# Routing tiles 0 to 3 early, so that expert 0's first block runs in fp32 beside the rest of the routing

## The reference

```
hx = rmsnorm(x) * (1 + scale1) + shift1        # adaLN; the same for the context
x  = x + gate1 * (concat(pool_mixer, gated_linear_attention) @ w_out)
hx = rmsnorm(x) * (1 + scale2) + shift2
s  = sigmoid(hx @ w_router)                    # 16 experts in 4 groups of 4
# the group with the best pair sum of s + router_bias is chosen, and in it the best 2 experts
dest: the token-expert pairs sorted by expert, each expert padded to whole blocks of 128 rows
for each block b of expert e:
    yb = (silu(xb @ w1[e]) * (xb @ w3[e])) @ w2[e]     # w1, w3: 1024 x 512; w2: 512 x 1024
x  = x + gate2 * (sum of a token's two rows of yb, weighted by s of the chosen two)
out = rmsnorm(x) * norm_f
```

## Time and profile before

| | us |
|---|---|
| median of three runs | 888.96 |
| the profiled execution | 889.26 |
| its span, from first to last instruction | 887.50 |
| PE busy (share of span) | 858.4 (97%) |
| DVE busy | 636.0 (72%) |
| ACT busy | 414.9 (47%) |
| POOL busy | 192.3 (22%) |
| mean granted clock of PE | 0.986 |

### The profile page before, as it was taken

How to read it: one execution, slowest core, us unless ns; L and a number is a source line. 1 busy time by engine, 2 the same in 40 slices (tenths; PEclk the granted TensorE clock), 3 DMA queues, 4 the chain that set the end, 5 groups by cost and what they waited for, 6 DMA issues and landing times.

```text
span 887.5 us, 14102 instructions
## 1 busy us (share of the span) xinstructions
PE 858.4 (97%) x4980; PEld 706.4 (80%) x4981; DVE 636.0 (72%) x907; ACT 414.9 (47%) x597; POOL 192.3 (22%) x225
## 2 busy tenths in 40 slices
PE   8999999999999999999799999999999999999993
PEld 6789878888997567887688888888888888888872
DVE  1578755789777748556985669399936648599995
ACT  3585456201224442222343456378634525487772
POOL 4042001100000101011032324133413222234324
PEclk9999999999999999999979999999999999999997
DMA  9953566511035032322789859979997596599994
GB/s 342 347 180 111 172 196 203 163 41 54 11 143 191 1 143 78 113 73 95 259 304 375 277 171 368 285 269 378 378 346 265 176 299 220 175 348 379 370 333 175
DMA packets 82358, 195.29 MB, mean 220 GB/s; under 512 B 4919, under 2 KB 13324, under 8 KB 82314
## 3 DMA queue, kind: packets, MB, share of 16 engines
q1 hardware_dynamic: 71168, 158.87, 50.2%
q0 software_dynamic: 8272, 25.84, 11.2%
q10 hardware_dynamic: 2874, 10.01, 2.9%
HBM read 169.57 MB, written 25.71 MB: 220 GB/s over the span
## 4 chain that ended last, share of the span: by engine, by line
PE 78%; DVE 11%; DMA 4%; issue 2%; ACT 2%; POOL 1%; ACTq 0%; SPq 0%; DVEq 0%; POOLq 0%
PE ps L2455 17%; PE ps L2443 12%; PE ps L2108 9%; PE ps L2460 8%; PE ps L2111 7%; PE ps L2437 2%; PE ps L2308 2%; DMA raw<-in_w_dram 2%; PE ps L2299 1%; DMA raw<-x_rows 1%; DVE arena L1423 1%; PE ps L2301 1%; PE ps L2300 1%; PE ps L2250 1%; PE ps L2164 1%
## 5 line engine op out<-in xcount | busy, mean ns | idle before, releaser
L1145 ACT ACTIVATE wah<-raw 128x2048 fp32r (+1 forms) x32 | 61.4, 1919 | 63.7 <-PE ps L2460 42.4
L1856 DVE TENSOR_TENSOR wbl<-raw,wbh 128x2048 fp32r<-128x2048 f32 x32 | 73.1, 2288 | 5.3 <-ACT wbh L1145 4.9
L2443 PE MATMUL ps<-w2h,hTh 128*128 128x512 f32 x184 | 76.1, 414 | 0.0
L2455 PE MATMUL ps<-wbh,xTh 128*128 128x512 f32 x184 | 73.9, 402 | 0.0
L2455 PE MATMUL ps<-wah,xTh 128*128 128x512 f32 x184 | 72.6, 394 | 0.0
L2443 PE MATMUL ps<-w2h,hTl 128*128 128x512 f32 x184 | 72.2, 393 | 0.0
L2455 PE MATMUL ps<-wal,xTh 128*128 128x512 f32 x184 | 72.2, 392 | 0.0
L776 POOL DMA_INDIRECT x_rows<-late_rows,block_dst x21 | 49.9, 2375 | 102.7 <-DVE late_rows L1871 102.7
L2443 PE MATMUL ps<-w2l,hTh 128*128 128x512 f32 x184 | 72.1, 392 | 0.0
L1856 DVE TENSOR_TENSOR wal<-raw,wah 128x2048 fp32r<-128x2048 f32 x30 | 68.8, 2292 | 4.5 <-issue 3.2
L1856 DVE TENSOR_TENSOR w2l<-raw,w2h 128x2048 fp32r<-128x2048 f32 x32 | 71.8, 2283 | 0.0
(11 more groups left out here) (412 smaller groups left out, 2173.8 us busy)
## 6 DMA issues: line engine op xcount, KB each, us to landing
raw<-in_w_dram SPq DMA_DIRECT2D x64, 1024.0 KB
raw<-in_w_dram SPq DMA_DIRECT2D x16, 2048.0 KB, 11.3
arena<-in_w_mod_dram SPq DMA_DIRECT2D x32, 512.0 KB, 4.0
arena<-in_x_dram SPq DMA_DIRECT2D x16, 512.0 KB, 9.5
arena<-in_w_mod_dram SPq DMA_DIRECT2D x3, 2048.0 KB, 13.9
arena<-in_w_in_dram SPq DMA_DIRECT2D x6, 1024.0 KB, 7.1
x_rows<-arena ACTq DMA_DIRECT2D x9, 512.0 KB, 3.0
hx_rows<-arena ACTq DMA_DIRECT2D x9, 512.0 KB, 4.5
```

The source lines that it names most:

```text
L1145: act.activation(high_half, raw_half, ACT.Copy).then_inc(w_high[j], 1)
L1856: dve.tensor_tensor(low_half, raw_half, high_half.bitcast(F32), ALU.subtract).then_inc(w_split[j], 1)
L2443: ins = pe.matmul(out_ap, parts[l][:, lhs], w_parts[w][:, cols], start=start and n == 0, stop=stop and n == 2)
L2455: pe.matmul(ps[:, 2 + j, :], xTh[:, k * P:(k + 1) * P], w[:, k * HALF:(k + 1) * HALF], start=(k == 0 and w is wh), stop=False)
```

## The change

Tiles 0 to 3 are routed for expert 0 one step earlier. `choose(0, 4)` moves from the end of step 7 to the end of step 6. New code on DVE and PE (`early_sums`, `early_ranks`, `early_places`, `early_list`, `early_tokens`) counts and places expert 0's tokens in these tiles and writes their numbers into `block_tok`. In step 7 POOL gathers their rows into `x_early`; in step 8 PE transposes them (`turn_early`) and ACT copies them to `xT_e`, both before tile 7's projection is finished. Block 0 holds these tokens and no others; expert 0's other tokens are numbered from block 1 on (`room_e` is added to the counts of tiles 4 and later).

Block 0 is computed in plain float32 from the loaded weights: four groups of four matmuls (`early_product`, units 0 and 1, for `w1` and `w3`), then eight for `w2`. They stand on PE where `keep_busy` stood: one group ahead of the ranks, two after them, one after the list of tokens. The `w2` matmuls have block 1's transposes between their halves. The weights are still split as before, for block 1. The matmuls for `slot_w` have their operands exchanged (32 x 128 in four groups of partitions, then a copy and one sum). The loops over blocks on PE, ACT and DVE begin one block later.

```diff
@@ sync, load_expert
-                        sp.wait_ge(S["gathered"], 16)
+                        sp.wait_ge(S["gathered"], 32)
...
+                    if first and n == 5:
+                        sp.wait_ge(S["l2_done"], 1)
@@ gpsimd
+                if t == NX - 1:
+                    for par in range(2):
+                        pool.wait_ge(hx2_stored[par], 16 * 2)
+                    pool.wait_ge(S["tok_ready"], 1)
+                    pool.indirect_dma_start(out=x_early, out_offset=None, in_=hx_dram[0:4 * P, :],
+                                            in_offset=bass.IndirectOffsetOnAxis(ap=block_tok[:, :], axis=0))\
+                        .then_inc(S["gathered"], 16)
...
-            gather(0, False)
+            gather(1, False)
@@ scalar
                 if t == NX:
+                    act.wait_ge(S["x_turned"], 1)
+                    act.activation(xT_e[:, :], ps[:, 0:2, :].rearrange("p h n -> p (h n)"), ACT.Copy).then_inc(S["xh_ready"], 1)
                     row_square(NX - 1, 0)
...
-            for k in range(2):
-                high(1, (k + 1) * UNIT, k)
+            high(1, UNIT, 0)
+            act.wait_ge(S["l1a"], 1)
+            act.activation(hsil[:, :], ps[:, 2, :], ACT.Silu).then_inc(S["silu_done"], 2)
+            high(1, 2 * UNIT, 1)
+            act.wait_ge(S["logit_parts"], NX + 1)
+            act.activation(hx2T[:, 0:P], ps[:, 5, 0:P], ACT.Copy).then_inc(S["logit_rows"], 1)
+            act.wait_ge(S["hta"], 1)
+            act.activation(hT_e[:, :], ps[:, 3, :], ACT.Copy).then_inc(S["hTh_a"], 1)
@@ vector
+            def early_sums():
+                mine = R["sel"][:, :, 0]
+                v(dve.tensor_tensor(R["two_of"][:, 0, :], mine[:, 1:8], mine[:, 0:7], ALU.add))
+                dve.tensor_tensor(R["four_of"][:, 0, :], R["two_of"][:, 0, 0:5], R["two_of"][:, 0, 2:7], ALU.add).then_inc(S["route_ready"], 1)
...
+                if t == NX - 1:
+                    early_places()
...
+                if t == NX - 2:
+                    v(dve.memset(R["sel"][:, 0:4, :], 0.0))
+                    early = choose(0, FIRST)
+                    next(early)
                 if t == NX - 1:
                     clear_counts()
-                    early = choose(0, FIRST)
-                    next(early)
...
-                if t == NX - 1:
+                if t == NX - 2:
                     for _ in early:
                         pass
+                    early_sums()
+                if t == NX - 1:
+                    early_tokens()
...
             first_low(0)
+            dve.wait_ge(S["silu_done"], 2)
+            dve.wait_ge(S["l1c"], 1)
+            dve.tensor_tensor(hid[:, :], hsil[:, :], ps[:, 4, :], ALU.mult).then_inc(S["hid_a"], 1)
@@ tensor
+            def early_ranks():
+                pe.wait_ge(S["on_ready"], 2 * (NX - 1))
+                pe.wait_ge(S["route_ready"], 1)
+                pe.matmul(ps[:, 2, 256:261], ones[:, :], rt["four_of"][:, 0, :], start=True, stop=False)
+                pe.matmul(ps[:, 2, 256:260], strict[:, :], rt["sel"][:, 4:8, 0], start=False, stop=True).then_inc(S["rank_done"], 1)
+            def turn_early():
+                pe.wait_ge(S["gathered"], 16)
+                for k in range(KC):
+                    ins = pe.transpose(ps[:, k // 4, (k % 4) * P:(k % 4 + 1) * P], x_early[:, k * P:(k + 1) * P], ident[:, :])
+                ins.then_inc(S["x_turned"], 1)
+            def early_product(unit, s_):
+                columns = raw[:, (unit + 1) * UNIT:(unit + 2) * UNIT].rearrange("p (k s n) -> p k s n", k=4, s=2)
+                for k in range(4):
+                    ch = 4 * unit + k
+                    ins = pe.matmul(ps[:, 2 + 2 * s_, :], xT_e[:, ch * P:(ch + 1) * P], columns[:, k, s_, :], start=(ch == 0), stop=(ch == KC - 1))
...
-            pe.wait_ge(S["rl_out"], NX)
-            keep_busy(8)
-            pe.wait_ge(S["route_ready"], 2)
+            pe.wait_ge(S["tok_ready"], 1)
+            pe.wait_ge(w_loaded[0], LOADS[0])
+            early_product(0, 0)
+            pe.wait_ge(S["route_ready"], 4)
...
-            keep_busy(20)
+            pe.wait_ge(S["small_ready"], 3)
+            early_product(0, 1)
+            pe.wait_ge(w_loaded[1], LOADS[1])
+            early_product(1, 0).then_inc(S["l1a"], 1)
```

More of the change, by code:

```diff
@@ L1174, in arrived @@
                 act.sem_inc(S["load_seen"], 1)
-            turn_out(0)
+            turn_out(1)
             act.wait_ge(S["table_ready"], 1)
             last = act.value_load(tabs[0:1, T_LAST:T_LAST + 1], min_val=NE - 1, max_val=MAXB - 1)
+            e, word = entry(act, 0)
+            with act.If(word > NE - 1):
+                place = [place_of(e, j) for j in range(3)]
+                arrived(0, e)
+                arrived(1, e)
+                for j in range(2):
+                    for k in range(2):
+                        act.wait_ge(w_split[j], k + 1)
+                        act.sem_inc(S["load_seen"], 1)
+                        high(j, place[k] * UNIT, k)
+                arrived(2, e)
+                for k in range(2):
+                    act.wait_ge(w_split[2], k + 1)
+                    act.sem_inc(S["load_seen"], 1)
+                    high(2, place[2] * UNIT, k)
             def block(b):
@@ L1213, in _ @@
             with act.Fori(0, NB // 4) as four:
[L1214 removed]
+                i = four * 4 + 1
                 with act.If(i < last):
@@ L1880, in _ @@
             first_low(1)
-            turn_out(0)
+            dve.wait_ge(S["rank_done"], 5)
+            v(dve.tensor_copy(slot_w[:, :], ps[:, 5, P:P + NB]))
             low(1, UNIT, 0, 0)
             low(1, 2 * UNIT, 0, 1)
-            dve.wait_ge(S["rank_done"], 3)
-            dve.tensor_copy(slot_w[:, :], ps[:, 5, 0:NB])
+            turn_out(1)
             dve.wait_ge(S["g2_loaded"], 16)
-            hidden(0, 0)
-            low(2, 3 * UNIT, 0, 0)
-            hidden_low(0, 0)
-            hidden(0, 1)
-            low(2, 3 * UNIT, 0, 1)
-            hidden_low(0, 1)
-            turn_out(1)
+            weigh(0)
             last = dve.value_load(tabs[0:1, T_LAST:T_LAST + 1], min_val=NE - 1, max_val=MAXB - 1)
             e, word = entry(dve, 0)
+            place = [place_of(e, j) for j in range(3)]
+            with dve.If(word > NE - 1):
+                for k in range(2):
+                    low(2, 3 * UNIT, 0, k)
+                for c in range(2):
+                    for k in range(2):
+                        low(c, place[k] * UNIT, e + 1, k)
+                for k in range(2):
+                    low(2, place[2] * UNIT, e + 1, k)
+                for k in range(2):
+                    hidden(1, k)
+                    hidden_low(1, k)
+            with dve.Else():
+                for k in range(2):
+                    hidden(1, k)
+                    low(2, 3 * UNIT, 0, k)
+                    hidden_low(1, k)
+            turn_out(2)
+            e, word = entry(dve, 1)
             place = [place_of(e, j) for j in range(3)]
@@ L2425, in _ @@
             ins.then_inc(S["rank_done"], 1)
+            early_product(1, 1).then_inc(S["l1c"], 1)
+            for n in ("l1a_half", "l1b"):
+                pe.sem_inc(S[n], 1)
             for part in range(2):
```

113 lines of the change are left out of this document (84 added, 29 removed).

## The result

The changed kernel takes 900.79 us (median of four runs, 899.51 to 901.15) against 889.13 of the kernel before on the same chip: 1.0129 of its time, 95% interval 1.0113 to 1.0145. It is slower by about 11.7 us. The forecast was 890.0 with a range of 885.0 to 893.6: the time lies above the range. The profiled execution took 899.51 us, the fastest of the four, with a span of 897.7, so 10.2 us more span than before; the medians are 1.4 us further apart than that.

A forecast was written before the change was run, and what follows sets the result against it. The prediction took PE, busy 97% of the span, to bound the kernel. Block 1 starting 3.7 us earlier and 4.7 us of clock loss gave +1.0 us on 888.96, so 890.0 us; range 885.0 to 893.6.

The forecast's parts named there:

- The step that failed: Blocks 1 to 22: unchanged, so the change is worth only how much earlier block 1 begins, 477.28 us before.
- the third rival: Blocks 1 and 2: expert 1's weights become late, price 0 to 3 us, time 891; chance 0.06.
- The stall at the early ranks: PE at 403.64 us: idle 4.0 us, waiting for DVE's choice and two sums in step 6.
- The wait for the gather: PE before the early transposes: waits 3.0 us, with 5.8 us from DVE's second list instruction to the first transpose.
- The clock: PE's queue before block 1: half rate in four places costs 1.2, 0.8, 2.0 and 0.7 us, together 4.7.
- half rate behind every wait: Slower rival, PE from early ranks to last matmuls before block 1: 8.5 us lost, time 893.8; chance 0.22.
- The third term: Clock loss behind PE's 5 us wait before the first product: 0 to 3.4 us, 2.0 taken.
- The load: Expert 0's first unit, before block 0's first product: issued behind tile 7's last projection at 435.5, landing at 445.1 us.
- The ranks: On DVE behind PE's first float32 product: ranks arrive at 449.6 us, 10.3 us late, before any clock loss.
- From the ranks to block 1: DVE's chain of 14.6 us and 9.4 us in series behind it: block 1 begins 24.0 us after the ranks.
- PE's own queue behind the ranks is shorter than that: Behind the ranks: PE's float32 groups and one-hot matmuls take 13.5 us, covered by DVE's chain of 14.6 us.
- The sum: Block 1's start: 3.7 us earlier without the clock, 4.7 us lost by the clock, together +1.0 us.

The follow-up runs named there:

- e1: Changed kernel with the splits of expert 1's weights on DVE put between the parts of block 1's own work again; 893.94 us, 1.0054 of the time before.
- e4: Changed kernel with the choice ending behind tile 7's masks, early ranks behind tile 6's projection, early list in tile 7's first half; 892.67 us, 1.0034 of the time before.
- e3: Changed kernel with the early rows' transposes and ACT's copy moved behind tile 7's last router sum; 896.16 us, 1.0080 of the time before.
- e5: Changed kernel with 100 unread matmuls of 128 columns ahead of PE's wait for expert 0's first load; 913.84 us, 1.0270 of the time before.
- e11: As e10, with 14 unread matmuls of 128 columns added ahead of the ranks; 881.82 us, 0.9912 of the time before.
- e12: As e11, with the load of expert 0's third unit issued only when its second has landed; 881.04 us, 0.9896 of the time before.
- e9: Changed kernel with 25 unread matmuls of 128 columns ahead of PE's wait for expert 0's first load; 900.48 us, 1.0118 of the time before.
- e6: Changed kernel with the load of expert 0's second unit issued only when its first has landed; 900.84 us, 1.0124 of the time before.
- e2: Changed kernel with block 0's first float32 product moved behind the ranks on PE; 899.46 us, 1.0112 of the time before.
- e10: Changed kernel with the edits of e1, e3, e4 and e2 together; 882.65 us, 0.9917 of the time before.

## Why the prediction was wrong, point by point

**The step that failed:** "The change leaves the number of blocks at 23 and blocks 1 to 22 as they are." DVE's code for block 1 stands ahead of the loop since the change, and its parts are in another order than in the loop's body: first all of block 1, then the six splits of expert 1. That cost 7.0 us from block 1's start to the last block's, 6.1 of them in block 2, and e1 gives 5.8 back. The forecast spoke of these splits only as a late load (the third rival, chance 0.06, up to 3 us). The place was right and the mechanism wrong: ACT's first split waited for PE, not for a load, and the loads, issued 17.6 us later than before, were in time. The last condition of the forecast, that a later block loses its pace, is the one that came true. The rest of the forecast was off by less: block 1 at 480.5 instead of the 478.3 forecast makes 890.0 + 2.2 = 892.2, inside the range. That is a sum and not a run. The run that comes nearest, e1, still pays 1.0 us in blocks 1 and 2 and measured 893.94, 0.3 above the range; so the time before block 1 alone brings the forecast to its upper edge, and the step on blocks 1 and 2 brings it well past.

**The stall at the early ranks:** 3.94 us, forecast 4.0. Shown by e4.

**The wait for the gather:** 2.30 us, forecast 3.0. From DVE's second list instruction (428.25) to the first transpose it was 5.5 us, 5.8 taken; the gather itself took 4.4 us to land.

**The clock.** Forecast 4.7 us in four places. Measured: 2.8 at the early ranks (1.2 taken; twelve matmuls in 5.15 us instead of 2.73, the ranks 0.84 instead of 0.43), some 1.5 behind the gather (0.8 taken; from there to the router's products 5.83 us, where e3 needs 3.35 and 1.0 for the transposes), 2.1 in the first product (2.0 taken), none in the `w2` product (0.7 taken). Together 6.4, each read in the one traced execution. The upper end of the first, 1.7, was too low: I had taken the one stretch at half rate of the earlier trace rows as the longest that there can be. The rival "half rate behind every wait" was the better description. The third term is real: in e5, e11 and e12, where the first product and the `w2` product both ran at full rate, block 1 begins 1.3 to 2.2 us sooner behind the landing than in the changed kernel. In e9 no gain of it reached the time.

The Trainium skill (TensorE: Matmul & The Clock Gate, section HAM oscillation — how this bites in real kernels) says that a kernel that waits for data between bursts starts each burst at half rate. The trace agrees after waits of 2.3, 3.9, 4.2 and 6.2 us in the changed kernel. In e11 the clock stayed at its upper level through waits of 1.7 and 1.1 us, and in e6 through one of 2.0 us. But gaps of 1 to 1.3 us came before the fall at 440 us in the kernel before, so no length of wait in these traces parts the two cases.

**The load.** From issue to the first product 10.9 us, 9.6 forecast. In e6, where no other unit was under way, it still took 10.3: from 440 to 448.8 us the core moved 2.6 MB, the 2.1 of the unit and 0.5 of the x rows stored beside it, at 294 GB/s on the average. The forecast had put its 9.6 together from 383 GB/s at first, 226 beside the store and 2 us until bytes flow; the sum was 1.3 us short.

**The ranks.** At DVE at 457.1, where 449.6 and 4.0 us of clock made 453.6: 2.4 us by the clock and 1.3 by the load, less 0.2 of smaller deviations.

**From the ranks to block 1:** 23.4 us, forecast 24.0 and 0.7. The number came out, and the reading behind it ("PE's own queue behind the ranks is shorter than that") only just: 13.5 against 14.6 us was a margin of 1.1, which is the wait at 471.71. As soon as the ranks move, PE's queue is the path. In nine of the kernels block 1 begins 30.0 to 30.9 us behind the landing, wherever the ranks stand. In e5, e11 and e12, in which all of it runs at full rate, it needs 27.8, 28.6 and 27.8 (in e5 the product stands behind the added matmuls, and the distance is from its start); in e6, where the second unit is late, 33.6.

**The sum.** 3.2 us later at block 1, instead of 1.0; 0.6 in block 1 and 6.1 in block 2, instead of none; 0.3 behind. 10.2 us, the difference of the spans.

**What stays open.** Why the `w2` product of block 0 runs in part at half rate in e2, e6, e9 and e10 (5.37 us) and not in the changed kernel and the eight others (3.67), behind the same two short waits of 1.06 and 0.59 us. There is one trace of each kernel, so this may be a matter of the execution and not of the kernel. The mean granted clock speaks for that: of the four executions of e10 one has 0.991 and took 880.57 us, the three others, the traced one among them, have 0.988 and took 882.42 to 883.31. It is not shown. The 1.4 us by which the medians differ more than the profiled executions are of the same kind: the traced execution of the changed kernel has 0.983 and 899.51 us, the three others 0.979 to 0.980 and 900.50 to 901.15. Where their clock was lower no trace shows.

## What to carry to other kernels

When an iteration is taken out of a loop and written ahead of it, compare its order on every engine with that of the loop's body: what counts is when the work for the next iteration starts, and a wait shows up one iteration later. Price a new wait of 2.3 us or more on the matmul engine with the wait and 1.5 to 2.8 us of half rate behind it; behind waits of 0.6 to 2.0 us these traces show both, a loss of 1.7 us and none. Before moving something past a wait, add up both chains from the wait to where they meet; where they differ by a microsecond, moving one shifts the bound and gains a microsecond at most. And compare the times of several executions before a trace of one is read as the kernel's: here they differed by up to 3.5 us.

## What the runs showed of the hardware that I had not expected

In the four places of the changed kernel's trace the loss by the clock does not grow with the wait: behind 2.3, 3.9, 4.2 and 6.2 us it was 1.5, 2.8, 1.8 and 2.1 us. A matmul of two float32 operands of 128 columns, repeated without a pause at full clock, took 0.226 us (100 in 22.6), as much as one F32R matmul of 512 columns (0.227 from start to start). A weight load was not held up by those issued behind it on the same queue: with the third held back, the second landed at 446.94 instead of 447.02, and with the second held back the first took 10.3 us, where it took 9.9 to 11.0 with all of them under way.
